# A pad of 192 bytes ahead of the matmul operands becomes 64 bytes

## The chip, the cores and the metric

The kernel runs on one NeuronCore of a Trainium2 chip. The metric is device time in microseconds of one execution; three executions of the kernel before took 4512.15, 4513.13 and 4494.66 us, with a median of 4512.15 us.

## The reference

The reference is a four-layer decoder followed by a two-layer conditional block, all in float32 on 256 tokens of width 1024. Cut to its frame:

```python
# first block: layers 0 and 3 RWKV-7, layer 1 stick-breaking attention, layer 2 top-k attention
for i in range(4):
    h = rms_norm(x, norm_mix[i])
    x = x + mixer(i)(h)                            # projections 1024x1024, scan or attention, output
    g, u = split(rms_norm(x, norm_ffn[i]) @ w_gu[i])
    x = x + (silu(g) * u) @ w_down[i]              # 1024 -> 2 x 2816 -> 1024
# second block, twice: x and ctx streams
x   = x   + 0.5 * mx[2] * ffn1(mod_norm(x));  ctx = ctx + 0.5 * mc[2] * ffn1(mod_norm(ctx))
x   = x   + mx[5] * (g0*conv + g1*gated_unit + g2*diff_attention + g3*conformer) @ w_o
x   = x   + 0.5 * mx[8] * ffn2(mod_norm(x))        # and the same for ctx in the first of the two layers
return rmsnorm(x, final_g)
```

## The kernel before

Activations lie in SBUF with the 1024 features as eight chunks of 128 partitions and the 256 tokens along the free axis, so a tensor of 1024 x 256 values takes 8192 bytes of each partition. All large matrices are streamed from HBM in panels of 128 x 1024 float32 values (512 KB). A ring of four slots holds them: SyncE issues the DMA into `raw` (`load_panel`, L495), ScalarE rounds it to a high part `whi` (`act_round`, L551), GpSimd computes the low part `wlo` = `raw` - `whi` (`pool_panels`, L541), and TensorE multiplies. The activations are split in the same way into a high and a low part. For each chunk of 128 features TensorE runs three matmuls of 128 x 128 weights by 256 moving columns: high by high, high by low, low by high (`pe_panels`, L638).

Which tile is the moving operand depends on the stage. Projections and the up half of each feed-forward block (FFN) read `AH` and `AL`; the down half of an FFN reads `HH` and `HL`; the four branch outputs of the second block read `BRH` and `BRL`. Value projections, which give tokens on partitions, swap the roles at L617: `AH` and `AL` are then the stationary operand and `whi` and `wlo` the moving one. There are eleven FFNs. Each has 22 steps of two panels in its up half (22 x 2 x 24 = 1056 matmuls) and 8 steps with 8, 8 and 6 chunks in its down half (8 x 22 x 3 = 528), 1584 matmuls in all.

Every engine has its own program, in the order of the code; semaphores order them. Nothing in the order depends on an address. Between FFNs stand norms, the RWKV scan with 64 x 64 matmuls, the attention stages and the convolutions, whose operands lie in the work tiles `W0` to `W8`, `scan`, `CTX` and `VF`.

The addresses are what the change touches. `sb(name, cols)` in `build` places a tile at the counter `place[0]` and moves the counter on by the tile's bytes rounded up to 64. `place[0] += n` between two calls leaves a gap of n bytes. By these lines the tiles start, in each partition, at these bytes:

| tiles | start before | start mod 256 | moved by the change |
|---|---|---|---|
| `raw0`, then eleven more ring slots, 4096 bytes each | 16512 | 128 | no |
| `X`, `CTX` | 65664, 73856 | 128 | no |
| `AH`, `AL` (and `scan`, `ada_tok` on the same bytes) | 82240, 90432 | 64 | yes |
| `cst` (the constant table) | 98688 | 128 | yes |
| `ones` | 114688 | 0 | yes |
| `STD`, `RSTD`, `silu`, `hid` | from 115264 | 64 | yes |
| `W0` to `W8`; `HH` on `W0` | 120384 | 64 | yes |
| `HL` | 142912 | 64 | yes |
| `VF`, small weight tiles, `BRH`, `BRL` | from 194112 | 64 | yes |

Of the kernel before, what the change touches and what calls it, by code (L numbers as in the profile page):

```python
# [215 lines left out]
def build(nc, a, out, CONST_AT):  # L216
# [3 lines left out]
    with ExitStack() as ctx:  # L220
        place = [-(-nc.sbuf_base // 64) * 64]

        def sb(name, cols, dt=F32, at=None):

            off = place[0] if at is None else at
            t = nc.alloc_sbuf_tensor_at(name, [P, cols], dt, offset=off)
            if at is None:
                place[0] += -(-cols * 4 // 64) * 64
            return t
# [11 lines left out]
        wlo = [sb(f"wlo{i}", SLOT, F32R) for i in range(RING)]  # L241
        X = sb("X", C * S)
        CTX = sb("CTX", C * S)
        place[0] += 192
        a_at = place[0]
        AH, AL = sb("AH", C * S, F32R), sb("AL", C * S, F32R)
        place[0] += 64
# [2324 lines left out]
```

## Time and profile before

| | |
|---|---|
| median of three executions | 4512.15 us (4494.66 to 4513.13) |
| the profiled execution | 4512.15 us, span 4510.3 us, so 1.85 us lie around the span |
| mean granted TensorE clock | 0.949 |
| TensorE busy with matmuls | 4057.2 us, 90% of the span |
| GpSimd busy | 2664.8 us, 59% |
| ScalarE busy | 1937.0 us, 43% |
| VectorE busy | 1601.6 us, 36% |
| DMA queue of the kernel | 661.06 MB, 50.7% of sixteen engines' span |

The busy shares are averages over stages of different kinds. Matmuls are pipelined: one is recorded as 0.28 us long while the next starts some 0.11 us later, so the busy time says that the engine never ran dry and not how fast it went. How fast it went is read from the number of matmuls in a stretch in which it was busy throughout.

### The profile page before, as it was taken

The page shows a single profiled execution, that of the slowest core. Times are in us where ns is not written, and L with a number is a line of the kernel's source. Part 1 is how long each engine was busy: PE and PEld are TensorE (multiplying, and loading weights), DVE is VectorE, ACT ScalarE, POOL GpSimd, SP SyncE. Part 2 cuts the span into 40 slices and gives each one's busy share as a digit, 9 for nine tenths or more (in the row PEclk, how much of TensorE's full clock was granted, in tenths as well). Part 3 has the DMA queues.
Part 4 walks back from the last instruction along what each step waited for, and adds up shares of the span by engine and source line. Part 5 has one row for each costly group of instructions (what it writes and reads, how often), then busy time and mean ns, then how long its engine had stood idle before and what let it go on. Part 6 is the DMA issues. An engine that isn't in the chain of part 4 may idle for free.

```text
span 4510.3 us, 94606 instructions
## 1 busy us (share of the span) xinstructions
PE 4057.2 (90%) x36305; PEld 3703.4 (82%) x36305; DVE 1601.6 (36%) x3002; ACT 1937.0 (43%) x2635; POOL 2664.8 (59%) x1186
## 2 busy tenths in 40 slices
PE   5899798899799889799999987999789999998799
PEld 5555798899589745499999977999689899987799
DVE  4533313413721453321212185215832212138421
ACT  3211445554344321154545454544545455446453
POOL 4001586486268500178778755777378787864576
PEclk8999899999899899999999998999899999999899
DMA  5345464365147334456556634555256565643454
GB/s 155 101 131 148 124 191 145 103 193 149 38 144 203 115 111 131 117 159 196 160 168 195 176 108 131 168 162 164 70 160 192 158 193 167 189 139 100 132 168 145
DMA packets 1177129, 664.73 MB, mean 147 GB/s; under 512 B 30141, under 2 KB 1138441, under 8 KB 1176743
## 3 DMA queue, kind: packets, MB, share of 16 engines
q1 hardware_dynamic: 1176871, 661.06, 50.7%
q8 instruction: 190, 3.11, 0.3%
q14 instruction: 68, 0.56, 0.0%
HBM read 659.92 MB, written 1.05 MB: 147 GB/s over the span
## 4 chain that ended last, share of the span: by engine, by line
PE 71%; issue 13%; POOL 7%; DVE 5%; ACT 2%; SPq 1%; DMA 1%; POOLq 0%; DVEq 0%; ACTq 0%
PE bank L638 54%; POOL wlo L541 7%; PE bank L967 6%; PE bank L718 2%; PE bank L617 1%; PE bank L1065 1%; PE bank L1059 1%; PE bank L801 1%; PE bank L1036 1%; DVE RSTD L724 1%; DVE W L740 1%; PE bank L874 1%; PE bank L1067 1%; PE bank L1042 0%; DVE AL L696 0%
## 5 line engine op out<-in xcount | busy, mean ns | idle before, releaser
L541 POOL TENSOR_TENSOR wlo<-raw,whi 128x1024 fp32r<-128x1024 f32 (+3 forms) x1182 | 2664.6, 2271 | 1821.4 <-ACT whi L551 1814.0
L638 PE MATMUL bank<-AH,whi 128*128 128x256 f32 x6320 | 1804.9, 286 | 193.9 <-DVE AL L696 104.9
L638 PE MATMUL bank<-AL,whi 128*128 128x256 f32 x6320 | 1787.2, 283 | 0.0
L638 PE MATMUL bank<-AH,wlo 128*128 128x256 f32 x6320 | 1785.4, 282 | 0.0
L551 ACT ACTIVATE whi<-raw 128x1024 fp32r<-128x1024 f32 (+3 forms) x1182 | 1173.2, 995 | 1162.7 <-PE bank L638 1010.2
L638 PEld LDWEIGHTS bank<-AH,whi 128*128 128x128 f32 x6320 | 1223.3, 194 | 212.7 <-issue 181.6
L638 PEld LDWEIGHTS bank<-AL,whi 128*128 128x128 f32 x6320 | 1225.6, 194 | 0.1
L638 PEld LDWEIGHTS bank<-AH,wlo 128*128 128x128 f32 x6320 | 1224.2, 194 | 0.0
L638 PE MATMUL bank<-HH,wlo 128*128 128x256 f32 x1936 | 537.0, 277 | 0.0
L638 PE MATMUL bank<-HH,whi 128*128 128x256 f32 x1936 | 537.0, 277 | 0.0
L638 PE MATMUL bank<-HL,whi 128*128 128x256 f32 x1936 | 537.0, 277 | 0.0
L787 DVE TENSOR_TENSOR bank<-silu,bank 128x256 f32<-128x256 f32 x242 | 103.8, 429 | 957.5 <-PE bank L638 957.5
L638 PEld LDWEIGHTS bank<-HH,wlo 128*128 128x128 f32 x1936 | 364.1, 188 | 0.0
L638 PEld LDWEIGHTS bank<-HH,whi 128*128 128x128 f32 x1936 | 364.1, 188 | 0.0
L638 PEld LDWEIGHTS bank<-HL,whi 128*128 128x128 f32 x1936 | 364.1, 188 | 0.0
L967 PE MATMUL bank<-raw,cond 128*32 128x512 f32 x576 | 270.4, 598 | 1.6 <-DMA raw<-in_w_ada 1.6
L769 ACT ACT_TABLE_LOAD x101 | 129.6, 1283 | 176.7 <-PE bank L638 176.7
L769 ACT ACTIVATE silu<-bank 128x256 f32<-128x256 f32 x242 | 93.1, 385 | 248.8 <-PE bank L638 247.7
L948 ACT ACTIVATE scan<-bank 128x256 f32<-128x256 f32 x80 | 30.7, 384 | 314.3 <-PE bank L1059 314.3
L967 PEld LDWEIGHTS bank<-raw,cond 128*32 128x32 f32 x576 | 52.0, 109 | 111.2 <-issue 96.4
L1141 DVE TENSOR_TENSOR scan<-scan,bank 128x256 f32<-128x256 f32 x80 | 33.7, 422 | 301.6 <-PE bank L1067 288.6
L684 DVE TENSOR_TENSOR X<-X,bank 128x256 f32 x64 | 27.0, 422 | 309.0 <-PE bank L638 309.0
(334 smaller groups left out, 4281.5 us busy)
## 6 DMA issues: line engine op xcount, KB each, us to landing
raw<-in_ffn_w SPq DMA_DIRECT2D x420, 512.0 KB, 3.9
raw<-in_w_in SPq DMA_DIRECT2D x182, 512.0 KB, 3.8
raw<-in_ffn_w_gu SPq DMA_DIRECT2D x176, 512.0 KB, 3.8
raw<-in_w_ada SPq DMA_DIRECT2D x144, 512.0 KB, 4.1
raw<-in_ffn_w_down SPq DMA_DIRECT2D x64, 512.0 KB, 4.2
raw<-in_rw_w_rkv SPq DMA_DIRECT2D x48, 512.0 KB, 4.2
raw<-in_ffn_w SPq DMA_DIRECT2D x56, 384.0 KB, 3.4
raw<-in_ds_w_in SPq DMA_DIRECT2D x28, 512.0 KB, 3.7
```

The lines of the kernel that those rows point to most:

```text
L541: pool.tensor_tensor(wlo[slot][:, 0:n], raw[slot][:, 0:n], whi[slot][:, 0:n], ALU.subtract).then_inc(lo_ready, 1)
L551: act.activation(whi[slot][:, 0:n], raw[slot][:, 0:n], ACT.Copy).then_inc(hi_ready, 1)
L617: mm = pe.matmul(ps, o, w, start=k == c == n == 0, stop=k == g.pps - 1 and c == nk - 1 and n == 2)
L638: mm = pe.matmul(ps[:, 0:o.shape[2]], w, o[:, k0 + c, :], start=tile not in started and c == n == 0, stop=last_panel and c == nk - 1 and n ...
L718: mm = pe.matmul(bank[4][:, 0:S], ones[:, :], W[8][:, c * S:(c + 1) * S], start=c == 0, stop=c == C - 1)
L724: dve.reciprocal(RSTD[:, :], STD[:, :]).then_inc(dve_step, 1)
L740: op = dve.scalar_tensor_tensor(h[:, o], x[:, o], gain(c), RSTD[:, :], ALU.mult, ALU.mult)
L769: act.activation(silu[j % 2][:, :], ps[:, 0:S], ACT.Silu).then_inc(silu_ready, 1)
L787: dve.tensor_tensor(hidden, silu[j % 2][:, :], banks[1][:, 0:S], ALU.mult).then_inc(bank_free, 2)
L801: mm = pe.matmul(bank[first + c // 2][:, (c % 2) * S:(c % 2 + 1) * S], mat, src[:, c * S:(c + 1) * S], start=True, stop=True)
L874: mm = pe.matmul(bank[4][base:base + m, 0:S], w3[:, c, 0:m], x[:, c * S:(c + 1) * S], start=c == 0, stop=c == C - 1)
L967: mm = pe.matmul(ps[32 * row:32 * row + 32, :], cond[:, 32 * c:32 * c + 32], raw[j][:, k * ADA_N:(k + 1) * ADA_N], start=c == 0, stop=c == ...
```

## The change

One number: the gap between `CTX` and `AH` shrinks from 192 to 64 bytes. `AH`, `AL` and every tile allocated behind them start 128 bytes lower; `raw`, `whi`, `wlo`, `X` and `CTX` stay. No instruction is added, removed or moved on any engine: the programs of all five engines are the same row by row (16750 rows on TensorE, 2132 on VectorE, 1556 on ScalarE, 866 on GpSimd, 1231 on SyncE), and only addresses in them differ.

```diff
         X = sb("X", C * S)
         CTX = sb("CTX", C * S)
-        place[0] += 192
+        place[0] += 64
         a_at = place[0]
         AH, AL = sb("AH", C * S, F32R), sb("AL", C * S, F32R)
         place[0] += 64
```

## Rows read from the trace of the kernel before

**Rows 1.** The page: busy time by engine, and the chain that ended last.
```profile
PE 4057.2 (90%) x36305; PEld 3703.4 (82%) x36305; DVE 1601.6 (36%) x3002; ACT 1937.0 (43%) x2635; POOL 2664.8 (59%) x1186
PE 71%; issue 13%; POOL 7%; DVE 5%; ACT 2%; SPq 1%; DMA 1%; POOLq 0%; DVEq 0%; ACTq 0%
```
**Rows 2.** Groups by line, TensorE: operation, tiles, count, busy us, mean ns.
```profile
L638 PE MATMUL bank<-AH,whi 128*128 128x256 f32 x6320 | 1804.9, 286 | 193.9 <-DVE AL L696 104.9 <-DVE AL L733 49.1 <-DVE AL L735 25.3
L638 PE MATMUL bank<-HH,whi 128*128 128x256 f32 x1936 | 537.0, 277 | 0.0
L638 PE MATMUL bank<-BRH,whi 128*128 128x256 f32 x240 | 76.4, 318 | 40.0 <-DVE BRL L696 18.2 <-DVE hid L2295 10.6 <-DVE W L2290 10.1
L617 PE MATMUL bank<-whi,AH 128*128 128x256 f32 x256 | 71.3, 279 | 0.0
```
**Rows 3.** Windows in FFNs, TensorE alone: stretch, us, busy (matmuls), clock, DMA.
```profile
595.00:675.00 80.00, 80.00 (x708) 1.00 0.65 190
...
2245.00:2325.00 80.00, 80.00 (x681) 1.00 0.63 184
2435.00:2515.00 80.00, 80.00 (x709) 1.00 0.67 195
...
3850.00:3930.00 80.00, 80.00 (x682) 1.00 0.64 186
4400.00:4480.00 80.00, 80.00 (x682) 1.00 0.63 184
```
**Rows 4.** Windows, the matmuls that read AH alone, up half of two FFNs.
```profile
2200.00:2240.00 40.00, 40.00 (x228) 1.00 0.63 182
2400.00:2440.00 40.00, 40.00 (x237) 1.00 0.68 199
```
**Rows 5.** Windows, the matmuls that read HH alone, down half of the same two.
```profile
2290.00:2330.00 40.00, 40.00 (x228) 1.00 0.66 191
2480.00:2520.00 40.00, 40.00 (x236) 1.00 0.67 194
```
**Rows 6.** Windows, matmuls of L617 alone (roles swapped).
```profile
740.00:760.00 20.00, 20.00 (x179) 1.00 0.65 195
...
2562.00:2571.00 9.00, 9.00 (x79) 1.00 0.76 218
```
**Rows 7.** Line L801, TensorE: count, duration ns min/median/max, first and last start us.
```profile
L801 PE MATMUL bank<-W,cst x234: 377/379/796, 157.0 to 4026.5; 128*128 128x256 f32 x117
...
L801 PE MATMUL bank<-W,ones x24: 379/379/483, 2722.8 to 4186.9; 128*128 128x256 f32 x24
```
**Rows 8.** Groups by line, VectorE: 256 columns with one operand in PSUM.
```profile
L787 DVE TENSOR_TENSOR bank<-silu,bank 128x256 f32<-128x256 f32 x242 | 103.8, 429 | 957.5 <-PE bank L638 957.5
...
L1141 DVE TENSOR_TENSOR scan<-scan,bank 128x256 f32<-128x256 f32 x80 | 33.7, 422 | 301.6 <-PE bank L1067 288.6 <-PE bank L1065 12.8
...
L684 DVE TENSOR_TENSOR X<-X,bank 128x256 f32 x64 | 27.0, 422 | 309.0 <-PE bank L638 309.0
...
L1143 DVE TENSOR_TENSOR scan<-scan,bank 128x256 f32<-128x256 f32 x64 | 26.5, 413 | 0.0
```
**Rows 9.** Waits: engine and line, who was waited for, us in total, times, longest.
```profile
POOL wlo L541 <- ACT whi L551: 1814.0, 620, 318.4
ACT whi L551 <- PE bank L638: 1010.2, 590, 19.9
...
PE bank L638 <- DVE AL L696: 104.9, 9, 18.8
...
PE bank L638 <- POOL wlo L541: 14.1, 11, 2.7
```
**Rows 10.** DMA issues: tiles, count, KB each, median us to landing.
```profile
cst<-in_const SPq DMA_DIRECT2D x1, 1664.0 KB, 6.8
...
W<-in_x SPq DMA_DIRECT2D x1, 1024.0 KB, 9.6
...
...
out<-W SPq DMA_DIRECT2D x2, 512.0 KB, 2.6
```

## Prediction

> **What bounds the kernel now.** I read the page first: TensorE is busy for 90% of the span and makes 71% of the chain that ended last; VectorE makes 5% of that chain, GpSimd 7%, ScalarE 2% [rows 1]. The waits say the same from the other side: GpSimd and ScalarE wait for each other and for TensorE by the thousand microseconds, while TensorE waits for `wlo` only 11 times, 14.1 us in all, and for the operand split of L696 104.9 us in 9 waits at the joints between stages [rows 9]. So the time is the matmul stream of L638 and L617 plus joints. The groups give its size: 3 x 6320 matmuls that read `AH` or `AL`, 3 x 1936 with `HH` or `HL`, 3 x 240 with the branch tiles and 3 x 256 at L617, 26256 in all [rows 2] (one form of each stands there, the other two have the same count).
>
> The change moves no instruction. What can change is how long an instruction takes at its new address, or who collides with whom. The measure for the largest part is the start-to-start interval of matmuls, so I cut 80 us out of each of the eleven FFNs, in which TensorE was busy for all 80. Eight of the eleven show 708 or 709 matmuls, three show 681 or 682; five of the eleven stand in [rows 3]. A window counts some two matmuls that only reach into it (0.28 us long, one each 0.11 us), so the intervals are 80 / 706 = 113.3 ns and 80 / 679.4 = 117.8 ns. The clock is 1.00 in all of them, so it isn't the clock. There are two paces, 4.4 ns or 3.9% apart, on the same instructions. Within an FFN the pace holds from the up half, which reads `AH`, into the down half, which reads `HH`: 228 then 228 in the slow one, 237 then 236 in the fast one [rows 4, 5]. It is a state that a stretch enters at its start and keeps, not a property of a tile.
>
> **Is the pace a matter of the address?** The change takes `AH`, `AL`, `HH`, `HL` and the branch tiles from 64 to 192 modulo 256, and leaves `whi` and `wlo` at 128. The moving operand's start less the stationary one's goes from 192 to 64 modulo 256. The trace of before holds three trials of this.
> First, L617 swaps the roles, so its moving operand lies 64 above the stationary one modulo 256, the distance that L638 will have. It shows the same two paces: 179 in 20 us is 20 / 176.6 = 113 ns, 79 in 9 us is 9 / 76.6 = 117.5 ns [rows 6].
> Second, modulo 512 the distance in L638 is 192 with `AH` (82240 - 32896) and 448 with `HH` (120384 - 32896). Both run at both paces [rows 4, 5].
> Third, L801 runs float32 matmuls with `W` moving and either `cst` (start 128 modulo 256) or `ones` (0 modulo 256) stationary, a relative shift by just the 128 bytes of this change: median 379 ns in both [rows 7].
> The mean of 286 ns with `AH` against 277 with `HH` and 318 with `BRH` [rows 2] looks like an effect of the tile. I don't count it: the two forms with the high mean are those with idle time before them, 193.9 and 40.0 us against 0.0 with `HH`, so they hold the first matmuls after each joint, and inside the stretches `AH` and `HH` run alike [rows 4, 5].
>
> **The sum.** Cost of the change for the matmul stream: 26256 x 0 ns = 0, by the three trials. Its bounds: if every stretch ran fast, the three slow FFNs would give back 3 x 1584 x 4.4 ns = 21 us, and if the other 26256 - 11 x 1584 = 8832 matmuls are slow in the same share, 3 of 11 (an estimate; outside the FFNs I have only short windows, one fast and one slow in [rows 6]), another 8832 x 3/11 x 4.4 ns = 11 us. That is 32 us below. If every stretch ran slow, 26256 x 4.4 ns = 116 us less the 32 already paid, 84 us above.
> VectorE and ScalarE work on the moved tiles: the nearest rows are one form of 256 columns with one operand in PSUM, on tiles at 128 (`X`, 422 ns) and at 64 modulo 256 (`scan` 422 and 413, the `silu` product 429) [rows 8]. The tile at another residue lies inside the spread of the others, so I take 0. The spread is 16 ns in 422, 3.8%; on the 7% of the chain that VectorE and ScalarE make it would be 4510 x 0.07 x 0.038 = 12 us, up or down. Nothing else hides it, as that 7% is on the path. GpSimd's operands (`raw`, `whi`, `wlo`) don't move: 0, and its cover, TensorE's 24 intervals per panel, stays. DMAs into moved tiles: the constant table and x at the start, the context rows, the small weight tiles, and the two stores of the result [rows 10]. The panel loads don't move. I take 0; if a row of 9.6 us changed by the same 3.8%, it would be 0.4 us.
> The Trainium skill (DMA: Bandwidth & Descriptors, How a descriptor splits into AXI transactions) says that a descriptor that doesn't start on a 256-byte boundary fetches from the boundary below it and pays for the unused bytes. By that rule a 4096-byte row that starts at 192 instead of 64 modulo 256 costs 134 beats instead of 130, an estimate of 3%: 0.1 us on the 2.6 us of each store of the result, which is read out of a moved tile [rows 10]. No run here shows the rule yet, and with it the sum would be 0.1 to 0.2 us instead of 0.
>
> Sum: the span of 4510.3 us and the 1.85 us around it, plus 0, is 4512.15 us. But the profiled execution had three slow FFNs by chance of the states, and another execution draws them anew. The three times of before, 4494.66, 4512.15 and 4513.13, are up to 18.5 us apart, which is the price of 2.6 slow FFNs at 1584 x 4.4 ns = 7.0 us each; the two paces are thus large enough to make that scatter. The profiled execution is the median of the three. I take their mean, 4506.6, as the middle of what the unchanged distribution gives, so 4507 us.
>
> **Rivals.**
> *The new distance keeps the stream at the fast pace.* Mechanism: the slow pace is a collision of weight reads and moving reads in SBUF that depends on the two starts, and 128 bytes takes them apart. For it: 4.4 ns more per matmul with equal instructions and clock needs some collision. Against it: both paces occur at every distance in the trace. Time: 4512 - 32 = 4480 us.
> *The new distance makes the slow pace usual.* The same mechanism on the other side, in the FFNs first, since they are 17424 of the matmuls. It decides once the slow FFNs are about six of eleven or more: (6 - 3) x 7.0 x 26256 / 17424 = 32 us, 4544. All slow it is 4512 + 84 = 4596 us. For it: the present mix is nearer the fast end (3 of 11), so there is more room above than below. Against it: L617 has that distance and isn't mostly slow in the two windows above.
> *An address effect outside the matmul stream*, on the VectorE and ScalarE instructions at the joints: 12 us either way, 4500 or 4524, which sits inside the scatter.
> *The change does nothing at all to addresses that matter* is the forecast itself; that the gap is rounded away is excluded, since 64 and 192 are both multiples of 64.
>
> **How the numbers follow.** Half a per cent, 22.6 us, is about what a measurement can tell from no change; that puts "same" between 4489.6 and 4534.7. The forecast (nothing but a new draw of paces) has 0.58, with a range of its own of 4490 to 4525. All or nearly all fast has 0.19, more slow stretches 0.20, the rest 0.03, inside. Of the forecast 0.03 falls below the bound by a lucky draw, and of the fast rival 0.03 stays above. Of the slow rival 0.18 lies beyond the upper bound, to which I add 0.05 for a distribution that is only moderately shifted or a cost that I haven't seen, taken from the forecast. So faster 0.19, same 0.58, slower 0.23. The range reaches down to 4478, just past the all-fast case, and up to 4556, about halfway into the slow rival; that leaves out about 0.05 below and 0.12 above.
>
> **What would show it.** In the changed kernel, windows of 80 us in each FFN should again read about 708 or about 681, with two to four of eleven at 681. All eleven at 708 is the first rival, seven or more at 681 the second. A third number (say 700, or 720) would mean that the address sets the interval itself, and that my reading of a state is wrong. L801's median should stay 379 ns, and the forms of VectorE that I compared should stay within 413 to 429 ns. The forecast is wrong if the time leaves 4490 to 4525 and the count of slow stretches explains it in every execution, not in one.

## The result and the profile after

The changed kernel took 4588.01 us (median of 4, 4582.72 to 4602.29) against 4512.64 us for the kernel before (4494.66 to 4544.62). The ratio is 1.0162 with a 95% interval of 1.0128 to 1.0196: slower by 1.6%. The forecast was 4507 us in a range of 4478 to 4556; the time lies outside, within the second rival ("the new distance makes the slow pace usual", up to 4596 us).

The page of the changed kernel: busy time by engine, and the chain by engine, to be held against [rows 1].

```profile
PE 4164.6 (90%) x36305; PEld 3797.8 (82%) x36305; DVE 1600.6 (35%) x3002; ACT 1935.0 (42%) x2635; POOL 2665.2 (58%) x1186
PE 71%; issue 13%; POOL 7%; DVE 5%; ACT 2%; SPq 1%; DMA 1%; POOLq 0%; DVEq 0%; ACTq 0%
```

TensorE is busy 107 us longer with the same 36305 matmuls; the other three engines have their old busy times to within 2 us, and the chain has the same shares. Only TensorE got slower. The windows in the FFNs say how; they answer to [rows 3] (columns as there, five of the eleven shown):

```profile
575.00:655.00 80.00, 80.00 (x681) 1.00 0.63 184
...
2265.00:2345.00 80.00, 80.00 (x682) 1.00 0.63 183
2460.00:2540.00 80.00, 80.00 (x681) 1.00 0.63 182
...
3900.00:3980.00 80.00, 80.00 (x682) 1.00 0.64 185
4455.00:4535.00 80.00, 80.00 (x682) 1.00 0.63 183
```

All eleven FFNs show 681 or 682, where the kernel before had eight at 708 or 709. There is no third number: the two paces, 113.3 and 117.8 ns, are the old ones, and the fast one is gone from the FFNs. Outside them short stretches of the changed kernel still run fast. The longest, a stretch that reads `AH` and `AL` at L638, takes 191 matmuls at 113.3 ns (TensorE alone, columns as above):

```profile
1600.00:1620.00 20.00, 20.00 (x179) 1.00 0.38 106
```

What the prediction compared beside the stream didn't move, by line L801 and by VectorE's forms ([rows 7, 8]):

```profile
L801 PE MATMUL bank<-W,cst x234: 377/379/796, 166.5 to 4119.3; 128*128 128x256 f32 x117
...
L801 PE MATMUL bank<-W,ones x24: 379/379/634, 2797.3 to 4283.6; 128*128 128x256 f32 x24
```

```profile
L787 DVE TENSOR_TENSOR bank<-silu,bank 128x256 f32<-128x256 f32 x242 | 103.9, 429 | 997.0 <-PE bank L638 997.0
...
L1141 DVE TENSOR_TENSOR scan<-scan,bank 128x256 f32<-128x256 f32 x80 | 33.7, 422 | 301.6 <-PE bank L1067 288.5 <-PE bank L1065 12.8
...
L684 DVE TENSOR_TENSOR X<-X,bank 128x256 f32 x64 | 27.0, 421 | 319.0 <-PE bank L638 319.0
...
L1143 DVE TENSOR_TENSOR scan<-scan,bank 128x256 f32<-128x256 f32 x64 | 26.5, 414 | 0.0
```

Medians of 379 ns and means of 413 to 429 ns as before; the growth at L787 and L684 is idle time in front of them (997.0 against 957.5 us, 319.0 against 309.0), VectorE waiting for a slower TensorE.

The account of the difference, from the start times of the records: between streamed matmuls at full clock lie 2886.1 us before and 2964.4 us after, for 25210 and 25211 intervals, 78.3 us of the 98.8 us by which the spans differ. Streamed matmuls at half clock give 2.7 us more, gaps in the stream 5.0 us less, everything else 22.8 us more. Much of the last part comes from that execution's own clock: outside the stream 417 intervals between matmuls lie at half clock, against 315 before, and the mean granted clock of the span is lower (4510.3 us at 0.949 before):

```profile
core 0: 4609.1 us, clock 0.944
```

The profiled execution after took 4610.93 us, 23 us above the median of its kernel. With medians the difference is 75 us, and the stream alone accounts for it.

### The profile page after: what moved, and what is told of

Read it like the earlier page. It is cut to its first block, busy times and chain, and to the rows that moved or that the text cites. A ratio compares the mean times of both kernels' runs of the same rounds, so it can differ in the third digit from the quotient of the medians.

```text
span 4609.1 us, 94606 instructions
## 1 busy us (share of the span) xinstructions
PE 4164.6 (90%) x36305; PEld 3797.8 (82%) x36305; DVE 1600.6 (35%) x3002; ACT 1935.0 (42%) x2635; POOL 2665.2 (58%) x1186
## 4 chain that ended last, share of the span: by engine, by line
PE 71%; issue 13%; POOL 7%; DVE 5%; ACT 2%; SPq 1%; DMA 1%; POOLq 0%; DVEq 0%; ACTq 0%
PE bank L638 54%; POOL wlo L541 7%; PE bank L967 5%; PE bank L718 2%; PE bank L617 1%; PE bank L801 1%; PE bank L1065 1%; PE bank L1059 1%; PE bank L1036 1%; DVE RSTD L724 1%; DVE W L740 1%; PE bank L874 1%; PE bank L1067 1%; PE bank L1042 0%; DVE AL L696 0%
## 5 line engine op out<-in xcount | busy, mean ns | idle before, releaser
L638 PE MATMUL bank<-AH,whi 128*128 128x256 f32 x6320 | 1817.8, 288 | 193.4 <-DVE AL L696 103.9
L638 PE MATMUL bank<-AL,whi 128*128 128x256 f32 x6320 | 1798.9, 285 | 0.0
L638 PE MATMUL bank<-AH,wlo 128*128 128x256 f32 x6320 | 1798.2, 285 | 0.0
L638 PEld LDWEIGHTS bank<-AH,whi 128*128 128x128 f32 x6320 | 1220.7, 193 | 212.0 <-issue 181.9
L638 PEld LDWEIGHTS bank<-AL,whi 128*128 128x128 f32 x6320 | 1224.2, 194 | 0.1
L638 PEld LDWEIGHTS bank<-AH,wlo 128*128 128x128 f32 x6320 | 1222.2, 193 | 0.0
L638 PE MATMUL bank<-HH,wlo 128*128 128x256 f32 x1936 | 541.0, 279 | 0.0
L638 PE MATMUL bank<-HH,whi 128*128 128x256 f32 x1936 | 540.8, 279 | 0.0
L638 PE MATMUL bank<-HL,whi 128*128 128x256 f32 x1936 | 540.5, 279 | 0.0
L787 DVE TENSOR_TENSOR bank<-silu,bank 128x256 f32<-128x256 f32 x242 | 103.9, 429 | 997.0 <-PE bank L638 997.0
L638 PEld LDWEIGHTS bank<-HH,wlo 128*128 128x128 f32 x1936 | 363.3, 188 | 0.0
L638 PEld LDWEIGHTS bank<-HL,whi 128*128 128x128 f32 x1936 | 363.2, 188 | 0.0
L638 PEld LDWEIGHTS bank<-HH,whi 128*128 128x128 f32 x1936 | 362.9, 187 | 0.0
L684 DVE TENSOR_TENSOR X<-X,bank 128x256 f32 x64 | 27.0, 421 | 319.0 <-PE bank L638 319.0
```

Source lines behind the costliest of these rows:

```text
L638: mm = pe.matmul(ps[:, 0:o.shape[2]], w, o[:, k0 + c, :], start=tile not in started and c == n == 0, stop=last_panel and c == nk - 1 and n ...
L787: dve.tensor_tensor(hidden, silu[j % 2][:, :], banks[1][:, 0:S], ALU.mult).then_inc(bank_free, 2)
```

## The experiments

All experiments move tiles and nothing else. "Distance" is the start of the moving tile less the start of the stationary tile (`whi` or `wlo`), modulo 256 bytes; it is 192 before and 64 after. Each kernel was timed against the kernel before on the same chip. The median of the kernel before was 4517.19, 4522.16, 4515.16 and 4516.20 us on the four chips of the experiments, so the ratios compare better than the times do. In the four kernels that move `wlo`, `X` and `CTX` lie behind it and move by the same bytes; no matmul of the stream reads them, and ring_up, where they move too, is as slow as the changed kernel. The table gives, beside the ratio, what the traces show in the eleven FFNs: matmul starts in 40 us of an up half and in 40 us of its down half (353 is 113.3 ns, 340 is 117.8 ns; these are starts, without the two or so that a window of the views counts on top, so 708 in 80 us of a view are 353 in 40 us here).

| kernel | whi to AH and HH | other | up / down halves, of eleven | us | ratio, 95% interval |
|---|---|---|---|---|---|
| before | 192 | | 8 at 353, 3 at 340 / the same | 4512.64 | 1 |
| changed | 64 | | all 340 / all 340 | 4588.01 | 1.0162, 1.0128 to 1.0196 |
| all_up | 192 | all tiles +128 | 10 at 353, 1 at 340 / the same | 4521.74 | 1.0007, 0.9986 to 1.0029 |
| ring_up | 64 | only ring, X, CTX moved | all 340 / all 340 | 4585.31 | 1.0153, 1.0118 to 1.0188 |
| pad448 | 192 | +256 | 8 at 353, 3 at 340 / the same | 4520.61 | 1.0015, 1.0001 to 1.0030 |
| pad128 | 0 | | 9 at 337, 2 at 334 / the same | 4624.96 | 1.0241, 1.0201 to 1.0281 |
| pad256 | 128 | | all 334 / all 333 | 4641.16 | 1.0278, 1.0241 to 1.0314 |
| pad160 | 160 | | 334 to 341 / the same | 4601.94 | 1.0174, 1.0131 to 1.0217 |
| pad224 | 224 | | 338 or 339 / 338 | 4611.03 | 1.0196, 1.0160 to 1.0232 |
| a_only | AH 64, HH 192 | | all 340 / 8 at 340, 3 at 353 | 4583.02 | 1.0138, 1.0100 to 1.0176 |
| rest_only | AH 192, HH 64 | | 9 at 353, 2 at 340 / all 340 | 4537.68 | 1.0027, 1.0004 to 1.0050 |
| wlo_up | 192 | wlo +128 | all 353 / all 353 | 4489.77 | 0.9942, 0.9922 to 0.9963 |
| both_up | 192 | wlo, AL, HL +128 | all 331 / all 331 | 4656.62 | 1.0307, 1.0279 to 1.0335 |
| al_up | 192 | AL, HL +128 | all 340 / all 340 | 4590.83 | 1.0154, 1.0106 to 1.0202 |
| wlo_up_gap192 | 64 | wlo at distance 192 | 8 at 353, 3 at 336 / the same | 4554.11 | 1.0081, 1.0050 to 1.0111 |
| wlo_up64 | 192 | wlo at distance 128 | all 338 / all 338 | 4601.69 | 1.0184, 1.0136 to 1.0232 |

**Distance or the tile's own start.** Two kernels cross the two.

```diff
+        place[0] += 128          # all_up: ahead of raw; the gap stays 192
         raw = [sb(f"raw{i}", SLOT) for i in range(RING)]
```

> All tiles, the ring included, start 128 bytes higher; the gap of 192 stays, so every distance between two tiles is that of before, while AH, HH and W start at 192 modulo 256 as in the changed kernel. Theory D (what counts is the distance from the stationary tile whi or wlo to the moving tile AH, AL, HH or HL, modulo 256): the paces of before, two to four slow FFNs of eleven, 4490 to 4545 us, ratio to before about 1.00. Rival A (what counts is where the moving tile itself starts, modulo 256): all FFNs slow, 4580 to 4600 us, ratio about 1.016.

```diff
+        place[0] += 128          # ring_up: ahead of raw
         raw = [sb(f"raw{i}", SLOT) for i in range(RING)]
-        place[0] += 192
+        place[0] += 64
         a_at = place[0]
```

> The ring, X and CTX start 128 bytes higher and the gap is 64, so AH and everything behind it lie exactly where they lay before, and only raw, whi, wlo, X and CTX have moved, to 0 modulo 256. Theory D (distance moving less stationary, now 64 modulo 256 as in the changed kernel): nearly all FFNs slow, 681 or 682 matmuls in 80 us, 4580 to 4600 us. Rival A (the moving tile's own start, now as before): 4490 to 4545 us.

Measured: all_up 1.0007, ring_up 1.0153. In ring_up no tile of the changed part moved at all, `AH` and `HH` lie where they lay before, and the loss is that of the change, its interval reaching over 1.0162. In all_up the tiles start at 192 modulo 256 as in the changed kernel, and the loss isn't there. Rival A is out: the distance counts, not the residue. One window of ring_up, then three of all_up, TensorE alone (stretch, us, busy, matmuls, clock, DMA):

```profile
4430.00:4510.00 80.00, 80.00 (x682) 1.00 0.63 185
```

```profile
550.00:630.00 80.00, 80.00 (x708) 1.00 0.65 190
2400.00:2480.00 80.00, 80.00 (x682) 1.00 0.63 184
4350.00:4430.00 80.00, 80.00 (x708) 1.00 0.66 192
```

The last FFN of ring_up is at 682, like its other ten; all_up has 682 in one FFN and 708 in the others. Which FFN is slow is another one than before (the sixth here; the fifth, tenth and eleventh before; the fourth, seventh and eleventh in pad448), so at distance 192 neither the distance nor the FFN fixes the pace. It looks drawn anew in each execution, though each kernel has one trace only.

**The curve over the distance.** Four kernels change only the number of the gap: 128, 256, 160 and 224 instead of 192. A fifth, with 448, keeps the distance modulo 256.

```diff
-        place[0] += 192
+        place[0] += 128          # pad128; 256, 160, 224 and 448 in the others
```

> Gap of 128 bytes: the moving tiles start at 128 modulo 256, distance 0 from whi and wlo. Theory D with a collision of two reads in step would make this the worst or the best distance; if the share of slow stretches goes smoothly from 192 (3 of 11) to 64 (11 of 11), distance 0 lies between or beyond: 4500 to 4600 us, paces still 113.3 and 117.8 ns. A third pace would show that the distance sets the interval itself. Rival A: residue 128 lies between 64 (before) and 192, 4510 to 4590 us.

> Gap of 256 bytes: the moving tiles start at 0 modulo 256, distance 128 from whi and wlo. Theory D: another point of the same curve, 4480 (all fast) to 4600 us (all slow), with the same two paces; a third pace would show that the distance sets the interval itself. Rival A: residue 0, on the other side of before, 4480 to 4545 us.

> Distance 160 modulo 256 (gap 160), between 128 (every matmul 120.0 ns, 4641 us) and 192 (mixed, 4515 us). Theory D: the time lies between these, 4515 to 4641 us, nearest guess 4575 us, or finds a pace of its own. If only a grid of 64 bytes counts, it equals one of its neighbours.

> Distance 224 modulo 256 (gap 224), between 192 (mixed, 4515 us) and 0 (118.9 ns, 4625 us). Theory D: between these, 4515 to 4625 us; if 192 isn't the best distance, all stretches at 113.3 ns and 4485 us, or a pace below it.

> Gap 448: the moving tiles start 256 bytes higher than before, distance still 192 modulo 256 but another one modulo 512. Theory D with a period of 256 bytes: as before, both paces in the FFNs, ratio 1.00, 4490 to 4545 us. Rival (the period is 512 or the whole address counts): anything else, up to the 4641 us of the worst gap.

Measured: 192 is the best of the six distances by 1.5% and more, and pad448 is the kernel before but for 0.15%. So the pattern repeats after 256 bytes, as near as these times tell. pad128 and pad256 took longer than the 4600 us at which their expectations ended, since the two-pace picture was too small: there are more paces. One window each of pad128, pad256 and pad224, and three of pad160:

```profile
560.00:640.00 80.00, 80.00 (x676) 1.00 0.62 181
```

```profile
4470.00:4550.00 80.00, 80.00 (x669) 1.00 0.62 182
```

```profile
565.00:645.00 80.00, 80.00 (x679) 1.00 0.62 181
```

```profile
570.00:650.00 80.00, 80.00 (x676) 1.00 0.62 182
930.00:1010.00 80.00, 80.00 (x685) 1.00 0.64 186
3700.00:3780.00 80.00, 80.00 (x669) 1.00 0.62 181
```

At distance 128 every matmul takes 120.0 ns (80 / 667), at 0 it is 118.7 in nine FFNs and 120.0 in two, at 224 118.3, and at 160 the eleven FFNs scatter over three paces, 117.3, 118.7 and 120.0. A step of 32 bytes from the best distance, to either side, costs as much as the 128 bytes of the change (1.0174 and 1.0196, the intervals overlap with its own). The fast pace appears in no FFN at any of the distances 0, 64, 128, 160 and 224.

A rival that no kernel was built for is that TensorE meets the reads and writes of the other engines. The intervals speak against it. In the fast FFNs of the kernel before they average 113.3 ns while a ScalarE instruction runs (3924 intervals) and while none does (4508), and the same under GpSimd (7400) and without it (1032). In pad256 all of these averages are 120.0 ns. Nor does the pace follow the DMAs: the fast stretch of the changed kernel shown above has a DMA share of 0.38, the fast FFNs before have 0.65 to 0.68. No kernel moved `raw` alone.

**The operand that is read, or a state that is kept.** The prediction had seen that an FFN keeps its pace from the `AH` half into the `HH` half. Two kernels set the halves apart.

```diff
-        place[0] += 192          # a_only: AH, AL moved, the rest not
+        place[0] += 64
         a_at = place[0]
         AH, AL = sb("AH", C * S, F32R), sb("AL", C * S, F32R)
-        place[0] += 64
+        place[0] += 192
```

> Gap 64 ahead of AH and 192 behind AL: AH and AL are at distance 64 modulo 256 as in the changed kernel, all tiles behind them (HH, HL, the branch tiles, W) where they were before, at distance 192. Theory D1 (the distance of the operands read decides at every moment): up halves at 681 matmuls in 80 us, down halves back at the fast pace; 18960 AH and AL matmuls go from 27% slow to all slow, 18960 x 0.73 x 4.4 ns = 61 us, the 5808 of the down halves give back up to 7 us, so 4565 to 4580 us. Rival D2 (the pace is entered at a stretch's start and kept): the down halves stay slow behind slow up halves, 4585 to 4600 us.

```diff
         AH, AL = sb("AH", C * S, F32R), sb("AL", C * S, F32R)
-        place[0] += 64           # rest_only: everything behind AL moved
+        place[0] += 192
```

> Gap 192 ahead of AH as before and 192 behind AL: AH and AL as before, all tiles behind them 128 bytes higher, at distance 64. Theory D1: down halves all slow, up halves mixed, 5808 x 0.73 x 4.4 = 19 us and the branch matmuls 2 us, 4525 to 4545 us. Rival D2: down halves keep the pace that the up half found, 4500 to 4530 us, with down halves at the fast pace behind fast up halves.

Two FFNs of rest_only, an up and a down half of each:

```profile
560.00:600.00 40.00, 40.00 (x356) 1.00 0.65 189
640.00:680.00 40.00, 40.00 (x342) 1.00 0.64 189
3440.00:3480.00 40.00, 40.00 (x342) 1.00 0.62 181
3520.00:3560.00 40.00, 40.00 (x342) 1.00 0.64 187
```

And two of a_only, again up and then down:

```profile
1375.00:1415.00 40.00, 40.00 (x342) 1.00 0.63 182
1445.00:1485.00 40.00, 40.00 (x355) 1.00 0.71 199
570.00:610.00 40.00, 40.00 (x342) 1.00 0.63 186
645.00:685.00 40.00, 40.00 (x342) 1.00 0.64 186
```

In rest_only a fast up half is always followed by a slow down half: as soon as the moving operand stands at distance 64, the fast pace is lost, in all nine FFNs that had it. In a_only the up halves are slow in all eleven, and behind them, back at distance 192, eight down halves stay slow and three recover. So both theories hold in part. At 64 an FFN runs slow whatever went before (D1). At 192 both paces occur, and a stretch mostly keeps the one it has (D2). But 64 doesn't exclude the fast pace, it makes it rare. Cut into blocks of 24 intervals, each called fast if it averages under 114.5 ns, the stream of L638 has 23 fast blocks of 972 in the changed kernel and 729 of 973 in the kernel before. ring_up, also at 64, has a fast stretch of 337 matmuls between two FFNs:

```profile
2624.00:2660.00 36.00, 36.00 (x320) 1.00 0.59 169
```

The traces show this, and the times add little: rest_only with 4538 us lies in D1's range, a_only with 4583 us between D1's 4565 to 4580 and D2's 4585 to 4600, and the kernel before was itself some 10 us slower on that chip than when the ranges were made.

**Which pair of reads.** A chunk issues three matmuls, `whi` with `AH`, `whi` with `AL`, `wlo` with `AH`, and in the records each load of weights starts with the matmul before the one it serves.

```diff
+        place[0] += 128          # wlo_up: ahead of wlo
         wlo = [sb(f"wlo{i}", SLOT, F32R) for i in range(RING)]
-        place[0] += 192
+        place[0] += 64
         a_at = place[0]
```

> 128 bytes more ahead of wlo and 64 ahead of AH: raw and whi as before, wlo at 0 modulo 256, all moving tiles as before. One of the three matmuls of a chunk reads wlo, so one of three pairs is at distance 64 and two at 192. Theory P (the collision is between a load of weights and the moving operand that is being read while it loads: whi under AH, whi under AH, wlo under AL) and theory Q (a matmul's own pair) both expect a change for one pair in three: slow in all stretches if a single pair at 64 suffices, 4575 to 4600 us, or a pace in between, 113.3 to 117.8 ns, 4520 to 4590 us.

both_up adds to this 128 bytes between `AH` and `AL`, and between `HH` and `HL`.

> As the kernel with wlo alone 128 bytes higher, and AL and HL 128 bytes higher too; whi, AH and HH as before modulo 256. Theory P (load of weights under the moving operand then being read): the pairs are whi under AH twice and wlo under AL, all at 192 again, so the time of before, 4490 to 4545 us. Theory Q (a matmul's own weights and its own moving operand): whi with AH 192, whi with AL 64, wlo with AH 64, so two pairs in three are at the slow distance and the time is 4575 to 4600 us, or above that of the kernel with wlo alone.

Measured: wlo_up 0.9942, both_up 1.0307. Neither theory had this. P expected both_up at the time of before, and it is the slowest kernel of all; Q expected wlo_up slower, and it is faster than both kernels of this study. One window of both_up, then four of wlo_up:

```profile
565.00:645.00 80.00, 80.00 (x664) 1.00 0.62 180
```

```profile
550.00:630.00 80.00, 80.00 (x708) 1.00 0.65 188
2200.00:2280.00 80.00, 80.00 (x708) 1.00 0.66 192
3795.00:3875.00 80.00, 80.00 (x708) 1.00 0.66 191
4340.00:4420.00 80.00, 80.00 (x708) 1.00 0.65 191
```

With `wlo` 128 bytes off the rest of its stream, all eleven FFNs run at 113.3 ns. Its five executions lie within 4486.64 to 4492.44 us, 6 us, where 14 of the kernel before on the same chip spread over 22 us. Three more kernels took the theories apart that were left.

```diff
         AH = sb("AH", C * S, F32R)
+        place[0] += 128          # al_up: between AH and AL; HL the same behind HH
         AL = sb("AL", C * S, F32R)
-        place[0] += 64
+        place[0] += 192
```

> 128 bytes more between AH and AL and between HH and HL, so AL and HL alone are 128 bytes off modulo 256; whi, wlo, AH, HH as before. Theory P' (pairs of a load and the moving operand under which it runs): whi under AH twice at 192, wlo under AL at 64, the same set as in the kernel with wlo alone moved, so all stretches fast, 113.3 ns, 4480 to 4500 us. Theory M (a jump of the moving stream by 128 bytes modulo 256 costs by itself, a jump of the weight stream doesn't): slower than before, 4560 to 4660 us, since AH to AL and AL to AH jump.

wlo_up_gap192 is wlo_up with the gap ahead of `AH` left at 192; wlo_up64 moves `wlo` by 64 bytes with a gap of 128.

> wlo 128 bytes higher, gap 192 kept: whi to the moving tiles 64 (as in the changed kernel), wlo to the moving tiles 192. Theory W (a jump of the weight stream keeps the stream out of the slow pace, wherever whi lies): fast, 4480 to 4520 us. Theory P'' (the distance from whi, which two loads in three read, decides): slow, 117.8 ns, 4575 to 4600 us.

> wlo only 64 bytes higher and gap 128: whi to the moving tiles 192 as before, wlo to them 128. Theory W or P'' (whi at 192 and wlo off it, in whichever direction): 113.3 ns or a little more, 4485 to 4530 us. Rival: it takes just the 128 bytes, and wlo at 128 under the moving operand costs a third of what the gap of 256 bytes cost, 4515 + 126 / 3 = 4557 us.

One window of al_up, two of wlo_up_gap192, one of wlo_up64:

```profile
560.00:640.00 80.00, 80.00 (x681) 1.00 0.63 184
```

```profile
555.00:635.00 80.00, 80.00 (x709) 1.00 0.65 191
1345.00:1425.00 80.00, 80.00 (x675) 1.00 0.62 181
```

```profile
560.00:640.00 80.00, 80.00 (x679) 1.00 0.62 182
```

al_up is slow in all FFNs and takes 4591 us, which is what M expected, although its set of pairs is that of wlo_up under P' and under Q. No sum over pairs explains both, so pairs alone are out. A jump by 128 bytes in the moving stream hurts (theory M; alone 1.0154, on top of `wlo`'s 1.0307 against 0.9942), a jump in the weight stream helps. It helps in wlo_up_gap192 too: `whi` is at distance 64 there, where no FFN of the changed kernel ran fast, and eight of eleven FFNs do. But three fall to a pace of 118.9 ns, and the time is 4554 us, which neither theory had named. The size of the jump counts: 64 bytes in place of 128 (wlo_up64) give 338 in 40 us everywhere, 118.2 ns, and cost 1.8%, more than both of its expectations. Other sizes weren't tried.

The pattern can be seen a second time where the roles are swapped. In al_up the three matmuls of a chunk in the value projections lie at distances 64, 64 and 192 with the jump in the stationary tile, just as L638 does in wlo_up_gap192, and their stretches run at the same two paces, 113.3 and 118.9 ns. Two windows on that line of al_up alone (L619 there):

```profile
2617.00:2625.00 8.00, 8.00 (x73) 1.00 0.73 211
1166.00:1175.00 9.00, 9.00 (x78) 1.00 0.01 2
```

**Open** is the mechanism underneath. That the two read streams of TensorE collide in SBUF, by something that repeats every 256 bytes, would explain why the distance counts, but no record shows a read. It doesn't explain by itself why one placement has two paces, or why a jump helps on one side and hurts on the other. The traces show only the start times.

## Why the prediction was wrong, point by point

*The bound* was right: the matmul stream sets the time, its chain share is the same after, and 78 of 99 us lie in it.

*The two paces* were right, with their sizes: 113.3 and 117.8 ns, 7.0 us per FFN. So was the price of the rival: 4596 us for all stretches slow, 4588 measured, by the ratio 1.6% where the rival had 84 / 4512 = 1.9%. A few short stretches of the changed kernel still run fast.

*The step that failed* is "Cost of the change for the matmul stream: 26256 x 0 ns = 0, by the three trials". What the trials could show and what I took from them differ in each.
- The first took L617, whose moving tile lies 64 above its stationary one, as a stand-in for L638 at 64. But it has other streams: there the moving operand goes `whi`, `wlo`, `whi` and the stationary one `AH`, `AH`, `AL`. In the changed kernel, where its distance is 192, it isn't steadier than it was at 64: three of its six longer stretches run fast and three slow, where it had been four and two. Here are the first, a fast one, and a slow one (matmuls of L617 alone):

```profile
765.00:782.00 17.00, 17.00 (x153) 1.00 0.63 194
...
2634.00:2643.00 9.00, 9.00 (x78) 1.00 0.75 218
```

  That is 17 / 150.6 = 113 ns and 9 / 75.6 = 119 ns (117.8 from the start times of the whole stretch). In wlo_up, where its moving stream jumps, all its stretches run at 117.8 ns. What a stretch with the roles swapped does at a distance doesn't settle what one without does: at distance 64 four of six longer stretches of L617 ran fast, and of L638 hardly any.
- The second compared distances modulo 512. It was right (pad448 confirms it), and beside the point, for the change moves the distance modulo 256, which was 192 in every stretch of L638.
- The third, L801, was right on itself (379 ns before and after). It is a float32 matmul with 216 ns from start to start in its records at full clock, and doesn't show what the 113 ns stream does. `W`, `cst` and `ones` also move together, so the row after doesn't test the change at all.

Over all three stood one wrong conclusion: both paces occur at this distance, so the distance doesn't matter. They occurred in a mixture, 8 to 3, and an address can set the mixture. rest_only and a_only show just that: at 64 no FFN half runs fast, at 192 most up halves of rest_only do. The blocks say it in one number: 75% of the stream of L638 was fast before, 2% after.

*VectorE, ScalarE, GpSimd, DMAs* at zero: right, by the rows after. The Trainium skill's rule on descriptors that don't start on a 256-byte boundary (DMA: Bandwidth & Descriptors, How a descriptor splits into AXI transactions) asked for some 0.1 us on each store of the result. The landing doesn't resolve it, 2.6 us before and after [rows 10]:

```profile
cst<-in_const SPq DMA_DIRECT2D x1, 1664.0 KB, 6.6
...
W<-in_x SPq DMA_DIRECT2D x1, 1024.0 KB, 9.3
...
out<-W SPq DMA_DIRECT2D x2, 512.0 KB, 2.6
```

The trace also holds the time of each of the 256 rows of 4096 bytes that the two stores send, and there the change shows: they average 158.9 ns before and 162.3 ns after, 2.2% more against the 3% that the rule gives. The eight traced kernels whose `W` starts at 64 modulo 256 have 157.9 to 159.5 ns, the four at 192 have 162.0 to 162.5. But pad256, whose rows start on the boundary and should be the cheapest by the rule, has 161.0 ns. So the rule has the sign and about the size of this change, and fails at 0. On a store of 2.6 us the 2.2% are less than 0.1 us.

*The draw of paces* as the source of the scatter between executions isn't shown. The FFNs that are slow do differ between kernels of one distance, and wlo_up, which has no slow FFN, scatters by only 6 us in five executions. But the changed kernel, with no fast FFN in its trace, lies between 4579.58 and 4610.93 us in thirteen executions, 31 us, where the kernel before spread over 22 to 43 us on the four chips of the experiments. So something else scatters the time too. The draw had a second meaning that I passed over. Before sat near the fast end of what can be, so a change without preference for a pace had more to lose than to win; I wrote that down and gave the slow rival 0.20.

## What to carry to other kernels

If one instruction runs at two paces in one trace with equal clock and operands, ask what selects the pace before calling it chance: that both occur says nothing on how often they will after the change. In a kernel bound by back-to-back float32r matmuls, the placement modulo 256 bytes of the stationary against the moving tiles is a parameter: one distance for all of them is worth 2.8% here (1 to 1.0278), and with `wlo` or `AL` and `HL` placed apart 3.7% (0.9942 to 1.0307). A gap that looks like leftover padding may carry it. It shows in one run per gap by counting matmuls in a fully busy window, which resolves 1% where the time of one execution scatters by as much.

## What the runs showed of the hardware

- The start-to-start interval of a 128 x 128 by 256-column float32r matmul at full clock in the FFNs was 113.3, 117.3, 117.8, 118.2 to 118.9, 120.0 or 120.9 ns on average, by nothing but tile placement. Shifting all tiles together by 128 bytes changed nothing (1.0007), shifting one side by 256 next to nothing (1.0015).
- At distance 192 the stream has two paces, and in all eleven FFNs of the kernel before it kept the one it had over the change from `AH` to `HH`. At distance 64 every FFN ran slow, and the fast pace came only in short stretches, 23 blocks of 972.
- The Trainium skill (SBUF — State Buffer, Who interferes with whom) gives TensorE two independent SBUF read ports, one for the moving operand and one for weights, and says that it never waits on another engine. The intervals, equal with the other engines busy and idle, agree with the second. Independent ports, taken at their word, would make tile placement free. Measured, it costs up to 120.9 against 113.3 ns per matmul, 6.7%, so for the distance between these two operands the measurement decides.
- Placing `wlo` another 128 bytes off, with every other operand of the stream as before, gave 4489.77 us, ratio 0.9942 (0.9922 to 0.9963): faster than both kernels.
